# Where the sums of weight pairs are formed in a two-layer decoder step: accumulating DMAs, or VectorE

## What is computed

```python
def conv_ffn(x, prev, w_gate, w_up, w_dw, w_down):
    g = x @ w_gate
    g_ext = jnp.concatenate([prev.astype(g.dtype), g], axis=1)
    g_c = depthwise_causal_conv(g_ext, w_dw)          # width 3, over tokens
    y = (jax.nn.gelu(g_c, approximate=True) * (x @ w_up)) @ w_down
    return y, g_ext[:, -(FFN_CONV_WIDTH - 1):]
```

## Time and profile before

| | us |
|---|---|
| median of 3 runs (3086.59 to 3092.24) | 3090.72 |
| the profiled execution, whole | 3088.02 |
| its span | 3086.3 |
| TensorE busy in it | 2984.7 |
| VectorE busy | 1901.5 |
| ScalarE busy | 1433.9 |
| first half of layer 0's FFN, up and down (403.74 to 793.78) | 390.04 |
| first half of layer 1's FFN, up and down (2324.67 to 2689.33) | 364.66 |
| paired turns of layer 1, 15.7 of them by their matmuls (2730.03 to 2896.05) | 166.02 |

### The profile page before, as it was taken

The page is one execution under the profiler, slowest core; times in us unless marked ns, Lnnn a source line. Parts: engine busy times, 40 slices in busy tenths (PEclk is TensorE's granted clock), DMA queues, the critical chain, the costliest instruction groups (busy, mean ns, idle before and its releaser), DMA issues.

```text
span 3086.3 us, 62600 instructions
## 1 busy us (share of the span) xinstructions
PE 2984.7 (97%) x24274; PEld 2589.4 (84%) x24274; DVE 1901.5 (62%) x2838; ACT 1433.9 (46%) x2709; POOL 497.8 (16%) x730
## 2 busy tenths in 40 slices
PE   8999999999999997999999999999999999999998
PEld 7887877787999896899777777777798888899998
DVE  6998677644676334633566666666657763577522
ACT  5344633233455232323477776777644333455422
POOL 0112100010000112231243343333200000000100
PEclk9999999999999998999999999999999999999999
DMA  4223899965686689986899999999745773488632
GB/s 130 72 84 102 228 247 272 271 199 148 223 289 216 211 221 234 248 251 176 310 375 406 399 401 402 397 403 396 266 143 185 242 238 110 127 291 274 210 108 86
DMA packets 560089, 739.66 MB, mean 240 GB/s; under 512 B 29185, under 2 KB 407418, under 8 KB 559720
## 3 DMA queue, kind: packets, MB, share of 16 engines
q1 hardware_dynamic: 511318, 589.87, 56.0%
q0 software_dynamic: 48384, 145.60, 17.2%
q10 hardware_dynamic: 92, 0.19, 0.0%
HBM read 624.99 MB, written 172.04 MB: 258 GB/s over the span
## 4 chain that ended last, share of the span: by engine, by line
PE 73%; DVE 10%; DMA 10%; issue 4%; ACT 3%; SPq 0%; POOL 0%; DVEq 0%; ACTq 0%; POOLq 0%
PE PS L1189 36%; PE PS L1643 11%; PE PS L2763 7%; PE PS L2799 4%; PE PS L2775 4%; DVE mT L992 4%; PE PS L2818 2%; DMA weight_sums<-in_ffn_w_up 2%; PE PS L2837 2%; PE PS L2828 2%; DMA raw<-in_ffn_w_down 2%; DVE wlo L417 2%; ACT whi L412 1%; DMA raw<-in_ffn_w_gate 1%; DMA raw<-in_ffn_w_up 1%
## 5 line engine op out<-in xcount | busy, mean ns | idle before, releaser
L417 DVE TENSOR_TENSOR wlo<-raw,whi 128x1024 fp32r<-128x1024 f32 (+1 forms) x300 | 359.4, 1198 | 619.5 <-ACT whi L412 611.4
L412 ACT CAST whi<-raw 128x1024 fp32r<-128x1024 f32 (+1 forms) x298 | 306.1, 1027 | 816.7 <-PE PS L1189 487.3
L1189 PE MATMUL PS<-xfh,whi 128*128 128x512 f32 (+3 forms) x1152 | 399.5, 370 | 30.2 <-DVE wlo L417 28.1
L1189 PE MATMUL PS<-xfl,whi 128*128 128x512 f32 (+3 forms) x1152 | 393.7, 365 | 0.0
L1189 PE MATMUL PS<-xfh,wlo 128*128 128x512 f32 (+3 forms) x1152 | 393.5, 364 | 0.0
L2763 PE MATMUL PS<-ident,kr 128*128 128x128 f32 x2048 | 277.2, 276 | 2.6 <-ACT kt L2933 2.6
L1189 PEld LDWEIGHTS PS<-xfh,whi 128*128 128x128 f32 x1152 | 210.1, 191 | 68.6 <-issue 33.8
L2763 PEld LDWEIGHTS PS<-ident,kr 128*128 128x128 f32 x2048 | 224.8, 141 | 39.1 <-issue 37.3
L3026 DVE COPY kt<-PS 128x512 f32<-128x512 f32 x256 | 172.6, 681 | 129.7 <-PE PS L2763 127.6
L1189 PEld LDWEIGHTS PS<-xfh,wlo 128*128 128x128 f32 x1152 | 209.6, 191 | 33.3
L1189 PEld LDWEIGHTS PS<-xfl,whi 128*128 128x128 f32 x1152 | 210.0, 191 | 32.8 <-issue 0.5
(11 more groups left out here) (446 smaller groups left out, 6673.6 us busy)
## 6 DMA issues: line engine op xcount, KB each, us to landing
kr<-in_cache_k SPq DMA_DIRECT2D x256, 512.0 KB, 7.7
vr<-in_cache_v SPq DMA_DIRECT2D x256, 512.0 KB, 7.4
raw<-in_ffn_w_down SPq DMA_DIRECT2D x64, 512.0 KB, 4.1
raw<-in_ffn_w_gate SPq DMA_DIRECT2D x54, 512.0 KB, 4.5
raw<-in_ffn_w_up SPq DMA_DIRECT2D x54, 512.0 KB, 4.0
extra_low<-weight_parts_kept SPq DMA_DIRECT2D x54, 512.0 KB, 5.7
weight_sums<-in_ffn_w_up POOLq DMA_DIRECT2D x24, 1088.0 KB, 8.9
weight_sums<-in_ffn_w_gate POOLq DMA_DIRECT2D x24, 1088.0 KB, 10.0
```

What stands on the lines that cost most here:

```text
L412: nc.scalar.copy(whi[b][:, 0:blocks_of(t), :], raw[t % RAWS][:, 0:blocks_of(t), :]).then_inc(w_hi, 1)
L417: nc.vector.tensor_tensor(wlo[t % RAWS][:, 0:n, :], raw[t % RAWS][:, 0:n, :], whi[b][:, 0:n, :].bitcast(F32), ALU.subtract).then_inc(w_lo, 1)
L1189: mm = nc.tensor.matmul(PS[:, s + c, 0:c1 - c0], stationary(wt, t, kw + k), x(k0 + k)[:, c0:c1], start=start and k == 0 and wt is whi and ...
```

## The change

The accumulating DMAs and the tensor `weight_sums` are gone. In the first half of each layer VectorE forms S1 and S3 of block f + 1 from the raw value tile and from a copy of gate low that ScalarE makes just before the gate tile is overwritten (`first_half_copy`); SP stores the pair (512 KB) to a new tensor whose rows are contiguous (2 KB to a partition for each sum, where the old one had 512 bytes to a row). In the paired blocks SP loads S1 and S3 from there, and gate low and gate high from the weights in the places of S2 and S4; VectorE adds S1 to gate low (S2) and S2 to gate high (S4) ahead of the splits. Two small copies (`fstg`) move from VectorE's `conv_taps` to ScalarE's `first_tap` in the paired blocks.

```diff
...
+    s_dram = nc.dram_tensor("weight_sums_kept", (NG, P, 2, HK, P), F32).ap()
...
-            for i in range(2 * KB):
-                pool.wait_ge(w_used, first["out00"] + i + 3)
-                weight_sum(pool, 0, i)
...
         def parts_kept(sp, layer, t):
...
+                if low and q == 1:
+                    f = FS0 + g
+                    sp.wait_ge(sg_s, SG_S + 2 * (NG * layer + g + 1))
+                    sp.dma_start(s_dram[g].rearrange("p a k m -> p (a k) m"), S13[f % 2]).then_inc(s_out[f % 2], 16)
...
                 if item in range(4):
-                    sp.dma_start(S_raw[item][s], cols(s_dram[layer, item], g, 0, HK)).then_inc(s_ld[item][s], 16)
+                    src = s_dram[g, :, item // 2] if item % 2 == 0 else cols(A["ffn_w_gate"][layer], f, HK * (item // 2), HK)
+                    sp.dma_start(S_raw[item][s], src).then_inc(s_ld[item][s], 16)
...
+        def weight_sum(dve, layer, g, item):
...
+            dve.wait_ge(s_ld[n][g % 2], S_LD + landed(layer, g))
+            if item == "S2":
+                dve.wait_ge(s_ld[0][g % 2], S_LD + landed(layer, g))
+                other = S_raw[0][g % 2]
+            else:
+                dve.wait_ge(sg_u, SG_U + u_count(layer, g, "S2"))
+                other = S_raw[1][g % 2]
+            nc.vector.tensor_tensor(S_raw[n][g % 2], other, S_raw[n][g % 2], ALU.add).then_inc(sg_u, 1)
...
+        def first_half_sums(dve, layer, f):
...
+            nc.vector.tensor_tensor(S13[f % 2][:, 0:HK], x[:, 0:HK], x[:, HK:KB], ALU.add).then_inc(sg_s, 1)
+            nc.vector.tensor_tensor(S13[f % 2][:, HK:KB], A11_kept[f % 2], x[:, 0:HK], ALU.add).then_inc(sg_s, 1)
+            dve.wait_ge(sg_s, SG_S + 2 * (NG * layer + f - FS0 + 1))
+
+        def first_half_copy(act, layer, f):
...
+            nc.scalar.copy(A11_kept[f % 2], raw[t % RAWS][:, 0:HK]).then_inc(sg_a, 1)
...
+            nc.scalar.copy(fstg[:, f, 0:2], gp[:, HP1:HP1 + 2])
+            nc.scalar.copy(fstg[:, f, 2:18].rearrange("p (b s) -> p b s", b=DB), samples_in(gp)[:, :, 4:6])
...
                 if g + 1 < NG:
+                    weight_sum(dve, layer, g + 1, "S2")
                     weight_low(dve, layer, g + 1, "S1")
...
                 if g + 1 < NG:
+                    weight_sum(dve, layer, g + 1, "S4")
                     weight_low(dve, layer, g + 1, "S2")
...
+                    if half == 0 and FS0 <= f + 1 < FS1:
+                        first_half_sums(dve, layer, f + 1)
                     next_lo(dve, t + 1)
...
-                    if half == 1:
-                        weight_sum(pool, 1, 2 * n)
-                        weight_sum(pool, 1, 2 * n + 1)
...
```

More of the change, by code:

```diff
@@ L1565, in landed, with sums_count, u_count @@
             return 16 * (sum(x % 2 == g % 2 for x in range(NG)) * layer + g // 2 + 1)
+        def sums_count(layer, f):
+            g = f - FS0
+            return S_OUT[f % 2] + 16 * (sum(x % 2 == f % 2 for x in range(FS0, FS1)) * layer + sum(x % 2 == f % 2 for x in range(FS0, f + 1)))
+        def u_count(layer, g, item):
+            return 2 * (NG * layer + g) + ("S2", "S4").index(item) + 1
         def parts_count(layer, f):
@@ L1616, in paired_sp @@
             if g == 0:
-                sp.wait_ge(sums_made, 16 * SUMS * (layer + 1))
+                for j in range(2):
+                    sp.wait_ge(s_out[j], sums_count(layer, FS1 - 2 + (FS1 - j) % 2))
                 sp.wait_ge(kept_out, rows_kept(layer))
@@ L2037, in up_dve @@
                 if half == 1 and f == FS0 - 1:
+                    weight_sum(dve, layer, 0, "S2")
                     weight_low(dve, layer, 0, "S1")
                 else:
+                    if half == 0 and FS0 <= f + 1 < FS1:
+                        dve.wait_ge(sg_a, SG_A + NG * layer + f + 1 - FS0 + 1)
                     next_lo(dve, t)
@@ L2060, in up_dve @@
                 if half == 1 and f == FS0 - 1:
+                    weight_sum(dve, layer, 0, "S4")
                     weight_low(dve, layer, 0, "S2")
                 else:
+                    if half == 0 and FS0 <= f + 1 < FS1:
+                        first_half_sums(dve, layer, f + 1)
                     next_lo(dve, t + 1)
@@ L2202, in down_pool @@
                     pool.dma_start(m_dram[n][:, 0:WID[half]], m_out[n % 2][:, 0:WID[half]]).then_inc(m_st[n % 2], 16)
-                    if half == 0 and layer == 0 and n < 5:
-                        weight_sum(pool, 0, 27 + n)
-                    if half == 1:
-                        weight_sum(pool, 1, 2 * n)
-                        weight_sum(pool, 1, 2 * n + 1)
         def parts_back_pool(pool, layer, half, k, ring):
@@ L2215, in parts_back_pool @@
             pool.dma_start(ring[k % 2][:, 0:WID[half]], m_dram[k][:, 0:WID[half]]).then_inc(m_ld[k % 2], 16)
-        def weight_sum(pool, layer, i):
-            gate, value = A["ffn_w_gate"][layer], A["ffn_w_up"][layer]
-            S1, S2, S3, S4 = (s_dram[layer, n] for n in range(4))
-            step, at_ = i // 4, CHUNK * (i % 4)
-            dst, src, row, add = ((S1, value, 0, False), (S3, gate, 0, False), (S1, value, HK, True), (S3, value, 0, True),
-                                  (S2, S1, 0, False), (S2, gate, 0, True), (S4, S2, 0, False), (S4, gate, HK, True))[step]
-            c0 = at_ + (FS0 * P if src is gate or src is value else 0)
-            to, of = dst[:, at_:at_ + CHUNK], src[row * P:row * P + HK * P, c0:c0 + CHUNK]
-            if SUMS * layer + i >= 1:
-                pool.wait_ge(sums_made, 16 * (SUMS * layer + i))
-            if add:
-                pool.dma_start(to, of, accum_op=ALU.add).then_inc(sums_made, 16)
-            else:
-                pool.dma_start(to, of).then_inc(sums_made, 16)
         def product_stored(pool, layer, f):
@@ L2239, in up_pool @@
         def up_pool(pool, layer, half):
-            if half == 0:
-                for f in range(FB):
-                    if layer == 0 and f % 2 == 1:
-                        pool.wait_ge(w_used, first["up00"] + 2 * f + 3)
-                        weight_sum(pool, 0, 16 + f // 2)
             if half == 1:
@@ L2406, in kv_pool @@
                     turn_pool(pool, i - 1)
-                if n % 2 == 0:
-                    weight_sum(pool, 1, 16 + KB * half + n // 2)
                 if half == 1 and 1 <= n <= KB:
```

28 lines of the change are left out of this document (22 added, 6 removed).

## The result

The changed kernel takes 3049.71 us in the median of 4 runs (3046.58 to 3051.02), the kernel before, measured beside it, 3089.72 (3086.59 to 3092.24): a ratio of 0.987, 95% interval 0.9852 to 0.9887. It is 40 us faster. The forecast was 3056, with a range of 3041 to 3076.

A forecast was written before the change was run, and what follows sets the result against it. The prediction took TensorE as the bound, busy 2984.7 of 3086.3 us. Gains of 53.9 us less costs of 4.8 (first halves), 10.5 (paired turns) and 4 (their starts) gave -34.6, so 3056 us against the median, range 3041 to 3076.

The forecast's parts named there:

- Where TensorE loses (first part): Whole kernel: TensorE is busy 2984.7 of 3086.3 us, so a change pays only where it closes a TensorE gap.
- Layer 0's first half: First half of layer 0's FFN: without the sums it takes layer 1's time, a gain of 25.4 us.
- Keys and values: Key and value projection: 19.6 us and 7.8 us lost in two windows, 27 us taken as the gain.
- Output projection: Layer 0's output projection, beside the first 16 sums: a gain of 1.5 us (0 to 3.3).
- First halves: FFN first half, each layer: 0.9 us for adds in block 7, 1.5 for stores; 4.8 us for both layers.
- Paired turns: Paired blocks: late gate low delays P6, costing 0.35 us a turn, 10.5 in all, plus 4 at the starts.
- Rival 1: Paired turns: the adds are hidden, the 10.5 us cost falls away, giving 3046 us; chance 0.20.
- rival 2: Paired turns: the loop takes its full price, 0.83 us a turn, 25 us, giving 3076 us; chance 0.14.
- rival 3: Keys and values: the gain is half, as another store on GpSimd's queue holds things up; 3069 us; chance 0.09.
- rival 4: Paired turns: gate low lands late every turn, costing 1.7 to 3.4 us each; 3097 to 3148 us; chance 0.04.
- rival 5: Layer 0's first half and the keys: the change does nothing, as they wait for something else; chance 0.03.
- the halved loop: Paired turns: with a queue-bound landing, P6 being 0.83 us late costs only 0.41 us a turn.

The follow-up runs named there:

- e8: Changed kernel plus layer 0's 32 accumulating DMAs at their old places, with the waits, into a tensor nobody reads; 3080.48 us.
- e6: Changed kernel plus layer 1's 32 accumulating DMAs at their old places, each waiting for the one before, into a tensor nobody reads; 3085.88 us.
- e7: As e6, but each DMA writes rows of its own and none waits for the one before; 3107.62 us.
- e1: Changed kernel with the add of S2 and split of S1 moved on VectorE from ahead of the gate to behind the convolution; 3028.03 us.
- e3: Changed kernel, but gate low is loaded to unread DRAM and VectorE adds S1 to itself, so the wait for the landing goes; 3029.25 us.
- e4: Changed kernel with the wait for gate low kept in place but the add of S2 behind it left out; 3038.82 us.
- e11: As e1, but first-half sum stores write 16 of 128 partitions, and paired blocks load value-weight quarters for S1 and S3; 3026.22 and 3028.56 us.
- e9: As e1, with the two small state copies of the paired blocks also moved back from ScalarE to VectorE; 3028.35 us.
- e10: As e1, but the two first-half adds in the turn of block 7 are left out in both layers; 3025.96 and 3026.9 us.

## Why the prediction was right

**Where TensorE loses (first part).** That a change pays only at TensorE's gaps held in every run. So did the two places.

**Layer 0's first half.** Taking layer 1 as the measure was right: -22.5 us against -23.0 with the stores and adds. e8 shows by itself that the DMAs are the cause, with 27.0 us. That is 1.6 more than the 25.4 taken; the stores of sums, which now share the stage with them, may be why, which no run separates.

**Keys and values.** That the DMAs are the cause is shown by e6; the size was too small: -33.4 us from the first matmul of `kv0` to the attention, where 27.4 had been worked out, and 1.5 more ahead of it. The step that failed is the choice of two windows of 40 and 20 us. Over the whole stretch (332.00 us before, 298.64 after) the rows are

```profile
1171.00:1503.00 332.00, 306.54 (x2041) 278.48 (x2042) 143.18 (x202) 97.17 (x134) 77.57 (x117) 0.96 0.85 234
```

and, after,

```profile
1153.00:1451.64 298.64, 297.79 (x2042) 271.89 (x2041) 142.37 (x201) 97.95 (x133) 59.79 (x98) 1.00 0.60 187
```

TensorE is idle 25.5 us in the one and 0.85 in the other, which is 24.6 of the 33.4; the other 8.8 are that the same 2041 matmuls were busy 306.5 us instead of 297.8, at a granted clock of 0.96 in place of 1.00. The two windows held 20.3 of the idle time and 7.1 of the clock's part. What was left out are gaps of 0.5 to 2 us in four other windows and the slower matmuls behind them. The explanation in that step, that the output blocks and keys queue behind the sums, named where the waits show, not what they cost: e7 took the waits out of GpSimd's queue, and keys, values and queries still took 335.6 us, against 337.3 with them and 298.6 without the DMAs.

**Output projection.** 1.0 us in the ledger, 0.6 by e8, 1.5 taken: within its bounds.

**First halves.** 2.3 us in layer 1 against 2.4. Inside it, block 7 costs 0.9 to 1.0, as worked out from VectorE's 10.48 busy of 10.91 us, and the second loss lies in the very turn that was named for it. The stores cost 0.5 to 0.8 where 1.5 was taken, and the sum is right only because 0.5 to 0.9 us more are lost for which nothing was taken; that part is luck.

**Paired turns.** The chain from the landing to P6 is what the trace of after shows, step by step, and e1, e3 and e4 show it by taking out its order, its landing and its add. In the profile of after the turns behind the start lose 5.6 to 5.7 us a layer, 0.40 each over 14 turns, where 0.35 was taken. They don't lose it evenly: in layer 1 they take between 10.53 and 12.25 us, and six of the 14 take 10.53 to 10.59, as before. The start loses 3.0 and 3.4 us where 2.0 was taken. Of that, P6 coming later is 1.7 us in layer 1 and 2.0 in layer 0, near the 2.0 worked out; the rest is the slower matmuls behind the gap, at a granted clock of 0.50 in the mean of 2.5 us, for which the sum had no term. Together it is 17.9 us in both layers against 14.5, and 13.4 to 17.9 in the four profiles of this code.

**The rivals.** Rival 1 (hidden) is refuted by the stages of 213 to 216 us, rival 2 by 0.40 in place of 0.83 a turn, rival 3 by 33 us where it had half of 27, rival 4, which needed 1.7 us or more in each turn, by the same 0.40, and rival 5 by e6 and e8, which bring both losses back. What speaks for the halved loop is the size alone, and as only about half of the turns lose anything it may have come near by luck; no run changed only the depth of the queue.

**The sum.** -34.6 predicted, -41.4 in the profiled executions. Of the 6.8 between them, 7.8 are the stage from block 20 to the attention, 3.3 the start and the end, which the change doesn't touch, and 3.4 in the paired turns go the other way; the rest cancels within 1 us. In the medians 6 us were missed. One reading in the working is off: VectorE is said to be through at 2831.11 + 0.64, where the row gives 0.72; nothing hangs on it, as gate low lands later.

**The rule that was weighed.** The Trainium skill, page "SBUF — State Buffer", section "A bandwidth-pool intuition that's wrong (but worth ruling out)", gives about 358 GB/s for a core to and from HBM. The slices of after stand at 387 to 405 GB/s through the attention, so the measurement again speaks against it as a ceiling. By that rule longer rows would bring nothing. In e1, with S1 and S3 in rows of 2 KB, they landed after 4.8 us in the median in one of the two slots and 4.4 in the other; in e11, with rows of 512 bytes, after 5.0 and 4.6. That looks like the 0.2 us guessed, but e9 and e10, with rows of 2 KB, have 5.0 and 4.3, and 4.6 and 4.6. So the 0.2 us is not shown, either way.

## What to carry to other kernels

Ask of every wait that a change adds what stands behind it on the same in-order engine, and write that chain down to TensorE with its durations: the add of 0.69 us was free wherever it stood behind the gate, and ahead of it, behind a landing, the add and its split cost 8 to 10 us a layer. Before you put a difference of a few us in one stage down to an edit, see how much that stage varies among kernels in which it is the same. Price a disturbed stage from its whole window, idle time and slower matmuls together, not from the largest gaps. When one queue's bulk transfers delay another's loads, take the order away and look before you blame it, and split the stage to see where the time went.

## What the runs showed of the hardware

Bulk DMAs from DRAM to DRAM delay other loads, and two at once do so more than one: the same number of transfers of 1088 KB made the stage 507.6 us long with waits and 530.7 without, against 467.7 with none, and the additional 23 us lie in `down01`, where two of them were under way together for 48 us (with blocks 20 and 21 it takes 195.1 us against 170.3, at 199 GB/s against 212). In the stretch behind it, where they ran one at a time but for its first 20 us, the waits made no difference (335.6 us without, 337.3 with). The two kernels also differ in where eight of the transfers read and in the rows that all of them write, which stays unseparated. A 512 KB load of key weights landed after 4.2 us in the median without them, after 7.2 and 7.3 with them and the waits, after 6.8 without the waits; single loads on e7's chain took 11 to 16. The mean DMA share of the stage was 0.81 in e6 and 0.78 in e7, at 225 and 215 GB/s, while the attention ran at 387 to 405: on the mean of the stage, the time was lost far below the rate that the core can move. In single windows the share stood at 0.92 to 0.99 at 224 to 313 GB/s.

TensorE's granted clock stayed at 1.00 behind a gap of 1.02 us and was 0.50 in the mean of the 2.5 us behind one of 2.56, which is the 1.2 GHz level, and 0.82 in the next 2.5 us.

e1_late is the best version found whose work is complete: 3028.03 us, 0.9806 of the kernel before (0.978 to 0.9833). e9_late_back can't be told from it.
